# A hybrid attention layer on one core: constants, a root and low parts moved between engines and later in their queues

## The chip, the cores and the metric

The kernel runs on one core of a Trainium2 chip. The metric is the device time of one execution in microseconds (us), taken as the median of several runs. The engines are TensorE (PE in the profile; PEld is its weight load), VectorE (DVE), ScalarE (ACT), GpSimd (POOL) and the queue that issues the transfers (SP). Each engine works through its own instructions in order and waits on semaphores for the others.

## The reference

One layer of a transformer with three kinds of attention side by side on the same normalised input of 1024 rows by 1024 columns, float32. Cut to what matters here:

```python
h = rmsnorm(x, norm_w) @ w_in                  # split into q, k, v and gates of three mixers
# A, differential attention, 4 heads: two softmax maps per head
a  = probs(q1, k1) - lam * probs(q2, k2)       # causal, with a distance penalty per head
oa = rmsnorm(a @ v, subln_w) * (1.0 - lam_init)
ya = oa * silu(ga)
# B, window of 128, 4 heads, with sinks
# C, sparse attention, 8 heads: compressed blocks, 8 chosen blocks of 64 keys, window of 512
oc = gates[..., 0:1] * o_cmp + gates[..., 1:2] * o_slc + gates[..., 2:3] * o_win
return rmsnorm(x + concatenate([ya, yb, yc]) @ w_out, final_norm)
```

## The kernel before

The program is a row of stages, each with its own instructions on every engine: start (normalisation and the first projections), `diff_phase` (A), `swa_phase` (B), the compressed branch of C, `nsa_phase` (window and chosen blocks of C, the last attention stage), and `out_phase` (output projection). Stages end with all engines together.

**High and low parts.** A float32 operand X of a matmul is held as a high part (X rounded to the matmul's format, made by ScalarE) and a low part (X minus the high part). Who makes the low part is a choice between VectorE and GpSimd.

**diff_phase.** A unit n is one head h and one block of 128 query rows; there are 32, eight to a head, and `pos` is n modulo 8. The blocks of a head come in the order 7, 3, 6, 2, 5, 1, 4, 0, so that the units of a head have 8, 4, 7, 3, 6, 2, 5, 1 key tiles of 128. For unit n, TensorE makes two score maps (`scores(n, 0)`, `scores(n, 1)`), VectorE adds the distance penalty and takes the negated maximum (`add_bias`, L837), ScalarE takes the exponentials (L775), VectorE combines both maps (`mix`, L846 to L849: a reciprocal, a small product, one scaled copy, one combination), TensorE transposes the result (`turn`, L657), ScalarE and VectorE copy it out in high and low parts (L785, L857), and TensorE multiplies with the values. Beside this, the `Filler` runs a quarter of an input projection in each unit up to unit 27: twelve matmuls of 512 columns (L169 to L171) whose weights come through a ring of two slots. Its weights are split by ScalarE (L146) and by `split_low` on GpSimd (L153), eight times in the stage: once at the beginning and after every fourth unit from n = 1. At `pos` 1 to 4 the stacks of the next head are made: ScalarE writes the high part (L768), VectorE the low part of the queries at `pos` 1 and 3 (L824), GpSimd the low part of the keys at `pos` 2 and 4 (L902).

TensorE's order in unit n is: `scores(n+2, 0)`, a quarter of the projection, `turn(n)`, `values(n-1)`, `scores(n+2, 1)`. VectorE's is: `add_bias(n+2, 0)`, `low_part(n)`, `mix(n+1)`, `add_bias(n+2, 1)`, then a stack. `scores(n, m)` waits until `add_bias(n-1, m)` has read the bank.

**nsa_phase.** A unit is a head, a branch and a block of query rows; there are 128, first eight of the window branch (at most five tiles), then eight of the chosen blocks (up to eight tiles), and so on. TensorE: `scores(n+2)`, `turn(n)`, `values(n-2)`; VectorE: `add_bias(n+2)` (L1668), `low_part(n)` (L1677); ScalarE: the exponential of unit n+1 (L1602), then `high_part(n)` (L1612). `scores(n)` waits for `add_bias(n-2)`. The first unit that uses the block mask (`n_blocks`), the second key stack (`stack(1)`: L1587 on ScalarE, L1642 on VectorE) and the full bias is n = 8. Ahead of its loop ScalarE has:

```python
exponentials(0)
stack(1)
act.wait_ge(consts_in, CONSTS)      # five transfers: bias, mask, sub-norm row, two gate tiles
nc.scalar.copy(blk[:, :], blk_in[:, :]).then_inc(mask_ready, 1)
```

The sub-norm of A is worked off in pieces in this stage: GpSimd squares (L1723), VectorE sums (L1648), ScalarE takes the root after unit 16 (L1596), VectorE the reciprocal after unit 18 (L1653, L1654), GpSimd scales (L1727, L1730).

## Time and profile before

| | |
|---|---|
| median of 3 runs | 933.0 us (932.86 to 935.32) |
| profiled execution, its own time | 934.59 us |
| its span, first to last instruction | 932.5 us |
| TensorE busy | 835.9 us (90%) |
| VectorE busy | 568.5 us (61%) |
| ScalarE busy | 432.5 us (46%) |
| GpSimd busy | 171.4 us (18%) |
| mean granted clock of TensorE | 0.946 |

Busy time is the time in which an engine has an instruction under way; the shares are means over stages that have different limits. In a group of instructions the number behind the x is how many there are; behind the first bar stand their busy time in us and the mean ns of one, behind the second the idle time of that engine just before them and what ended most of it. In a timeline the first two columns are start and duration in us, and a bracket at the end of a row is the idle time of the engine before it and what ended it. The granted clock is 1.00 at 2.4 GHz and 0.50 at 1.2 GHz.

### The profile page before, as it was taken

Reading aid. Unit: us, or ns where it says so; the run is one execution under the profiler, and the core shown is the slowest. Engines: PE = TensorE matmul, PEld = TensorE weight load, DVE = VectorE, ACT = ScalarE, POOL = GpSimd, SP = SyncE. Lnnn points to the kernel's source line nnn. Section 1 sums busy time; section 2 is a strip of 40 time slices with the busy share of each in tenths; the row PEclk is TensorE's granted clock in tenths of the full one; section 3 lists DMA queues with packets and bytes.
Section 4 is the critical chain, followed back from the end, with each engine's and each line's share of the span. In section 5 each row is a group of like instructions: output and inputs, shape, how many; then the busy total and the mean of one; then the engine's idle time right before and its main releaser. Section 6 shows DMA issues by size and latency. Waiting matters only on the chain. (4 is left out here: it accounts for less than half of the span.)

```text
span 932.5 us, 19153 instructions
## 1 busy us (share of the span) xinstructions
PE 835.9 (90%) x7748; PEld 706.9 (76%) x7748; DVE 568.5 (61%) x1305; ACT 432.5 (46%) x969; POOL 171.4 (18%) x123
## 2 busy tenths in 40 slices
PE   3999999969898888689889993989999999979997
PEld 3899887757686767578778872878887988868885
DVE  4841111136989888567639982878787877843332
ACT  5621111034565555357433322677777787732221
POOL 0233000030312231021045310141010323031220
PEclk9999999989899999699979995999999999979999
DMA  7220226052314122061254316000001111032431
GB/s 267 101 114 1 73 97 169 12 148 82 97 64 123 36 91 69 27 174 44 68 134 107 91 46 174 2 2 2 3 2 47 47 48 47 3 113 94 133 135 45
DMA packets 31942, 73.04 MB, mean 78 GB/s; under 512 B 5104, under 2 KB 13680, under 8 KB 30832
## 3 DMA queue, kind: packets, MB, share of 16 engines
q1 hardware_dynamic: 31856, 71.83, 24.8%
q8 instruction: 61, 1.00, 0.5%
q14 instruction: 25, 0.20, 0.1%
HBM read 55.57 MB, written 16.25 MB: 77 GB/s over the span
## 5 line engine op out<-in xcount | busy, mean ns | idle before, releaser
L1677 DVE SCALAR_TENSOR_TENSOR n_probsT_low<-n_turned,n_probsT_high 128x512 f16<-128x512 f32 (+3 forms) x192 | 94.4, 520 | 32.1 <-ACT n_probsT_high L1612 29.8
L1602 ACT ACTIVATE n_probs<-n_probs,n_negated_max 128x640 f32<-128x640 f32 (+7 forms) x128 | 94.0, 734 | 26.4 <-DVE n_negated_max L1668 25.7
L1612 ACT ACTIVATE n_probsT_high<-n_turned 128x512 f16<-128x512 f32 (+3 forms) x192 | 81.1, 457 | 37.7 <-PE n_turned L657 35.4
L657 PE MATMUL n_turned<-identity,n_probs 128*128 128x128 f32 x528 | 82.2, 280 | 16.1 <-ACT n_probs L1602 15.7
L1770 PE MATMUL n_scores<-w_and_keys_high,stacks 128*128 128x256 f32 (+2 forms) x192 | 78.5, 409 | 3.9 <-DVE n_negated_max L1668 2.5
L657 PEld LDWEIGHTS n_turned<-identity,n_probs 128*128 128x128 f32 x528 | 61.0, 143 | 23.7 <-ACT n_probs L1602 17.9
L153 POOL TENSOR_TENSOR w_and_keys_low<-w_raw,w_and_keys_high 128x1024 fp32r<-128x1024 f32 x15 | 38.2, 2546 | 154.1 <-ACT w_and_keys_high L146 153.9
L1771 PE MATMUL n_scores<-w_and_keys_low,stacks 128*128 128x256 f32 (+2 forms) x192 | 63.2, 336 | 0.0
L1668 DVE CUSTOM_DVE_ANT_0 n_probs<-n_scores,n_bias_full 128x1024 f32<-128x1024 f32 (+3 forms) x64 | 48.3, 754 | 20.0 <-PE n_scores L1774 19.9
L580 PE MATMUL nat<-stacks,xT_high 128*128 128x256 f32 (+1 forms) x192 | 56.0, 292 | 2.8 <-DVE stacks L452 2.6
L785 ACT ACTIVATE a_probsT_high<-a_turned 128x512 f16<-128x512 f32 (+3 forms) x48 | 21.8, 489 | 74.0 <-PE a_turned L657 74.0
L581 PE MATMUL nat<-stacks,xT_high 128*128 128x256 f32 (+1 forms) x192 | 55.2, 287 | 0.0
L582 PE MATMUL nat<-stacks,xT_low 128*128 128x256 f32 (+1 forms) x192 | 55.1, 287 | 0.0
L1969 PE MATMUL o_acc<-stacks,o_yT_high 128*128 128x512 f32 x128 | 51.8, 404 | 2.7 <-POOL o_yT_low L1942 2.7
L1745 POOL TENSOR_TENSOR branches_b_c<-branches_b_c,n_out 128x512 f32<-128x512 f32 x16 | 20.4, 1274 | 179.9 <-DVE n_out L1689 179.9
L169 PE MATMUL a_projected<-xT_high,w_and_keys_high 128*128 128x512 f32 x128 | 52.2, 408 | 0.7 <-ACT staged L179 0.7
L170 PE MATMUL a_projected<-xT_low,w_and_keys_high 128*128 128x512 f32 x128 | 52.0, 406 | 0.0
L171 PE MATMUL a_projected<-xT_high,w_and_keys_low 128*128 128x512 f32 x128 | 51.7, 404 | 0.0
L1970 PE MATMUL o_acc<-w_out_low,o_yT_high 128*128 128x512 f32 x128 | 50.9, 398 | 0.0
L1971 PE MATMUL o_acc<-stacks,o_yT_low 128*128 128x512 f32 x128 | 50.9, 398 | 0.0
L775 ACT ACTIVATE branches_b_c<-branches_b_c,a_negated_max 128x1024 f32<-128x1024 f32 (+7 forms) x64 | 49.4, 774 | 0.4 <-DVE a_negated_max L837 0.4
L665 PE MATMUL n_outp<-values_b_and_selected,n_probsT_high 128*128 128x64 bf16 x864 | 48.6, 193 | 0.0
(266 smaller groups left out, 2540.8 us busy)
## 6 DMA issues: line engine op xcount, KB each, us to landing
w_raw<-in_w_feat SPq DMA_DIRECT2D x23, 512.0 KB, 3.7
features<-staged SPq DMA_DIRECT2D x30, 256.0 KB, 2.0
a_raw<-features SPq DMA_DIRECT2D x36, 128.0 KB, 2.7
s_raw<-features SPq DMA_DIRECT2D x18, 256.0 KB, 4.3
branches_b_c<-in_x SPq DMA_DIRECT2D x8, 512.0 KB, 5.1
silu_gates<-staged SPq DMA_DIRECT2D x16, 256.0 KB, 2.0
gatesT<-silu_gates SPq DMA_DIRECT2D x8, 512.0 KB, 5.4
keys_and_w_out_raw<-in_w_out SPq DMA_DIRECT2D x4, 1024.0 KB, 4.8
```

The lines of the kernel that those rows point to most:

```text
L169: self.nc.tensor.matmul(bank[:, :], a, self.xh[:, k, cols], start=(k == 0), stop=False)
L170: self.nc.tensor.matmul(bank[:, :], a, self.xl[:, k, cols], start=False, stop=False)
L580: nc.tensor.matmul(nat[n % 4][:, 0:cols], xh[:, k, part], a[:, k, 0:cols], start=(k == 0), stop=False)
L581: nc.tensor.matmul(nat[n % 4][:, 0:cols], xh[:, k, part], b[:, k, 0:cols], start=False, stop=False)
L582: mm = nc.tensor.matmul(nat[n % 4][:, 0:cols], xl[:, k, part], a[:, k, 0:cols], start=False, stop=(k == KT - 1))
L657: mm = nc.tensor.transpose(dst[:, j, :], src[:, c:c + P], ident[:, :])
L1602: nc.scalar.activation(pr[:, n % PS, 0:w], pr[:, n % PS, 0:w], ACT.Exp, scale=-1.0, bias=nmax[:, hb % 4, qt:qt + 1], accum_out=sums[:, hb ...
L1612: nc.scalar.activation(pth[:, g % GS, 0:k, :], tp[g % TS][:, 0:k, :], ACT.Copy, scale=PSCALE).then_inc(t_high, 1)
L1677: nc.vector.scalar_tensor_tensor(out=ptl[:, g % GS, 0:k, :], in0=tp[g % TS][:, 0:k, :], scalar=PSCALE, in1=pth[:, g % GS, 0:k, :], op0=ALU ...
L1770: nc.tensor.matmul(out, q, kh[br][:, keys], start=True, stop=False)
L1771: mm = nc.tensor.matmul(out, q, kl[br][:, keys], start=False, stop=not masked)
L1969: nc.tensor.matmul(acc[n % 4][:, :], yh[:, i % 2, k, :], wh[:, k, cols], start=(k == 0), stop=False)
```

## The change

It has four parts. (1) In `diff_phase` GpSimd has no work left: its eight `split_low` become `split_low_on_vector`, the first ahead of everything VectorE does in the stage, the others at the end of the unit after the one in which ScalarE splits; its six key stacks become `stack_keys`, at the end of units with `pos` 2 and 4, on VectorE. (2) In `nsa_phase` ScalarE goes straight into its loop; `stack(1)` moves behind unit 1 (on VectorE too) and the mask copy behind unit 4. (3) The transfers that the mask copy waits for are three instead of five: the two gate tiles count to the semaphore of the output weights, and mask, bias and sub-norm row are issued ahead of the loads of the last two key stacks. (4) The square root on ScalarE and the reciprocal on VectorE go; VectorE makes the reciprocal root by an integer estimate and three Newton steps, twelve instructions on 128x32 elements, after unit 16.

```diff
--- before.py
+++ after.py
@@ -144,6 +145,14 @@
             act.wait_ge(self.sig.loaded, 16 * (self.loads + j - 1))
             act.wait_ge(self.sig.done, self.before + 2 * (j - 1))
         self.nc.scalar.copy(self.ring.hi[:, (self.first + j) % 2, :, :], self.ring.raw[:, :, :]).then_inc(self.sig.high, 1)
+
+    def split_low_on_vector(self, dve, j):
+        if not self.has(j):
+            return
+        s = (self.first + j) % 2
+        dve.wait_ge(self.sig.high, self.splits + j)
+        self.nc.vector.tensor_tensor(self.ring.lo[:, s, :, :], self.ring.raw[:, :, :],
+                                     self.ring.hi[:, s, :, :].bitcast(F32), ALU.subtract).then_inc(self.sig.low, 1)
 
     def split_low(self, pool, j):
         if not self.has(j):
@@ -824,6 +833,12 @@
                 nc.vector.scalar_tensor_tensor(out=low, in0=raw_of(j)[A_QK:2 * A_QK, :], scalar=A_QK ** -0.5 / slope4(h),
                                                in1=low.bitcast(F32), op0=ALU.mult, op1=ALU.subtract).then_inc(q_ready, 1)
 
+            def stack_keys(j):
+                h, m = j // LOADS, j % LOADS // 2
+                dve.wait_ge(stack_high, j + 1 - LOADS)
+                low = ks[2 * A_QK:K, 2 * (h % 2) + m, :]
+                nc.vector.tensor_tensor(low, raw_of(j)[2 * A_QK:K, :], low.bitcast(F32), ALU.subtract).then_inc(k_ready, 1)
+
             def add_bias(n, m):
                 w = len(tiles[n]) * P
                 at = score_layout(len(tiles[n]))[0]
@@ -858,6 +873,7 @@
                                                    in1=pth[:, g % GS, 0:k, :], op0=ALU.mult,
                                                    op1=ALU.subtract).then_inc(t_low, 1)
 
+            fill.split_low_on_vector(dve, 1)
             lc = Chain(dve, chain)
             dve.wait_ge(lam_loaded, 64)
             for i in range(2):
@@ -892,23 +908,10 @@
                     add_bias(n + 2, 1)
                 if pos in range(1, LOADS, 2) and h + 1 < A_H:
                     stack(LOADS * (h + 1) + pos - 1)
-
-        @block.gpsimd
-        def _(pool):
-            def stack(j):
-                h, m = j // LOADS, j % LOADS // 2
-                pool.wait_ge(stack_high, j + 1 - LOADS)
-                low = ks[2 * A_QK:K, 2 * (h % 2) + m, :]
-                nc.gpsimd.tensor_tensor(low, raw_of(j)[2 * A_QK:K, :], low.bitcast(F32), ALU.subtract).then_inc(k_ready, 1)
-                pool.wait_ge(k_ready, (j + 1 - LOADS) // 2)
-
-            fill.split_low(pool, 1)
-            for n in range(UN):
-                h, pos = n // NT, n % NT
-                if split_at(n):
-                    fill.split_low(pool, split_at(n))
                 if pos in (2, 4) and h + 1 < A_H:
-                    stack(LOADS * (h + 1) + pos - 1)
+                    stack_keys(LOADS * (h + 1) + pos - 1)
+                if n >= 1 and split_at(n - 1):
+                    fill.split_low_on_vector(dve, split_at(n - 1))
 
         @block.tensor
         def _(pe):
...
@@ -1502,9 +1505,10 @@
     PS, TS, GS = 4, 3, 6
     GU = RC * HU
     SLABS = 3
-    CONSTS = 16 * 5
+    CONSTS = 16 * 3
+    MASK_AT = 4
     SPLIT_AT = (GU + 8, GU + 24, 6 * HU + 4)
-    ROOT_AT = 2 * NT
+    RSTD_AT = 2 * NT
     yc = yr[:, 2:6, :].rearrange("p a n -> p (a n)").rearrange("p (t d) -> p t d", t=NT)
     qs, gate = stacks, glog
     with ExitStack() as ctx:
...
@@ -1564,19 +1569,19 @@
 
             sp.dma_start(bw[:, :], dist_win).then_inc(bw_in, 16)
             load_stack(1)
+            sp.dma_start(blk_in[:, :], blocks).then_inc(consts_in, 16)
             sp.dma_start(bf[:, :], dist_full).then_inc(consts_in, 16)
-            sp.dma_start(blk_in[:, :], blocks).then_inc(consts_in, 16)
+            sp.dma_start(sub[:, :], subln.partition_broadcast(P)).then_inc(consts_in, 16)
             load_stack(2)
             load_stack(3)
-            sp.dma_start(sub[:, :], subln.partition_broadcast(P)).then_inc(consts_in, 16)
             for i in range(2):
-                sp.dma_start(gates[:, i, :, :], gate_dram[:, :, i * P:(i + 1) * P].rearrange("k p n -> p k n")).then_inc(consts_in, 16)
+                sp.dma_start(gates[:, i, :, :], gate_dram[:, :, i * P:(i + 1) * P].rearrange("k p n -> p k n")).then_inc(w_loaded, 16)
             sp.wait_ge(k_ready, 3)
             for s in range(SLABS + 1):
                 if s >= 1:
                     sp.wait_ge(w_low, s)
                 sp.dma_start(raw[:, :, :], w_out[s]).then_inc(w_loaded, 16)
-            sp.wait_ge(w_loaded, 16 * (SLABS + 1))
+            sp.wait_ge(w_loaded, 16 * (2 + SLABS + 1))
 
         @block.scalar
         def _(act):
@@ -1587,13 +1592,9 @@
                 nc.scalar.copy(kh[j % 2], raw[:, j % 2, :]).then_inc(stack_high, 1)
 
             def split(s):
-                act.wait_ge(w_loaded, 16 * (s + 1))
+                act.wait_ge(w_loaded, 16 * (2 + s + 1))
                 act.wait_ge(scored, GU if s < 2 else 6 * HU)
                 nc.scalar.copy(stacks[:, 2 * s:2 * s + 2, :], raw[:, :, :]).then_inc(w_high, 1)
-
-            def a_roots():
-                act.wait_ge(a_vector, 3)
-                nc.scalar.activation(arms[:, :], arms[:, :], ACT.Sqrt, scale=small[:, 1:2], bias=small[:, 2:3]).then_inc(a_root, 1)
 
             def exponentials(n):
                 w = len(tiles[n]) * P
@@ -1613,17 +1614,17 @@
                                          scale=PSCALE).then_inc(t_high, 1)
 
             exponentials(0)
-            stack(1)
-            act.wait_ge(consts_in, CONSTS)
-            nc.scalar.copy(blk[:, :], blk_in[:, :]).then_inc(mask_ready, 1)
             for n in range(UN):
                 if n + 1 < UN:
                     exponentials(n + 1)
                 high_part(n)
+                if n == 1:
+                    stack(1)
+                if n == MASK_AT:
+                    act.wait_ge(consts_in, CONSTS)
+                    nc.scalar.copy(blk[:, :], blk_in[:, :]).then_inc(mask_ready, 1)
                 if key_stack_at(n):
                     stack(key_stack_at(n))
-                if n == ROOT_AT:
-                    a_roots()
                 if n in SPLIT_AT:
                     split(SPLIT_AT.index(n))
 
@@ -1649,9 +1650,14 @@
                                         ALU.add).then_inc(a_vector, 1)
 
             def a_rstd():
-                dve.wait_ge(a_root, 1)
-                ch.link(nc.vector.reciprocal(arms[:, :], arms[:, :]))
-                nc.vector.tensor_scalar(arms[:, :], arms[:, :], small[:, 3:4], None, ALU.mult).then_inc(a_vector, 1)
+                v, r, t = arms[:, :], guess[:, 0, :], guess[:, 1, :]
+                ch.link(nc.vector.tensor_scalar(v, v, small[:, 1:2], EPS, ALU.mult, ALU.add))
+                ch.link(nc.vector.tensor_scalar(r.bitcast(I32), v.bitcast(I32), -0.5, 1597463007.0, ALU.mult, ALU.add))
+                for _ in range(3):
+                    ch.link(nc.vector.scalar_tensor_tensor(out=t, in0=v, scalar=-0.5, in1=r, op0=ALU.mult, op1=ALU.mult))
+                    ch.link(nc.vector.tensor_tensor(t, t, r, ALU.mult))
+                    ch.link(nc.vector.scalar_tensor_tensor(out=r, in0=t, scalar=1.5, in1=r, op0=ALU.add, op1=ALU.mult))
+                nc.vector.tensor_scalar(v, r, small[:, 2:3], None, ALU.mult).then_inc(a_vector, 1)
 
             def add_bias(n):
                 w = len(tiles[n]) * P
@@ -1691,21 +1697,21 @@
 
             add_bias(0)
             add_bias(1)
-            stack(1)
             ch.link(nc.vector.tensor_scalar(small[:, 0:1], lam_size[:, :], 1.0 / PSCALE, None, ALU.mult))
             ch.link(nc.vector.tensor_tensor(small[:, 1:2], small[:, 0:1], small[:, 0:1], ALU.mult))
             ch.link(nc.vector.tensor_scalar(small[:, 1:2], small[:, 1:2], 1.0 / HD, None, ALU.mult))
-            ch.link(nc.vector.tensor_scalar(small[:, 3:4], small[:, 0:1], 0.5 * (1.0 - LAM_INIT), None, ALU.mult))
-            nc.vector.memset(small[:, 2:3], EPS).then_inc(a_vector, 1)
+            ch.link(nc.vector.tensor_scalar(small[:, 2:3], small[:, 0:1], 0.5 * (1.0 - LAM_INIT), None, ALU.mult))
             for n in range(UN):
                 if n + AHEAD < UN:
                     add_bias(n + AHEAD)
                 low_part(n)
+                if n == 1:
+                    stack(1)
                 if key_stack_at(n):
                     stack(key_stack_at(n))
                 if n in (NT, NT + NT // 2):
                     a_sums((n - NT) // (NT // 2))
-                if n == ROOT_AT + 2:
+                if n == RSTD_AT:
                     a_rstd()
                 if n % NT == 2 and n > NT:
                     write_out(n // NT - 1)
...
```

The order of VectorE's instructions in `diff_phase` around the end of unit 2, before the change. `ISA` with `a_scores` is `add_bias`; `a_probsT_low` is `low_part`; the four rows from the reciprocal are `mix(4)`.

```order
L837 ISA branches_b_c,a_negated_max<-a_scores,a_bias 128x768
L837 ISA a_negated_max 128x1
L837 ISA branches_b_c,a_negated_max<-a_scores,a_bias 128x256
L837 ISA a_negated_max 128x1
L857 SCALAR_TENSOR_TENSOR a_probsT_low<-a_turned,a_probsT_high 128x384
L846 RECIPROCAL a_sums<-a_sums 128x2
L847 TENSOR_TENSOR a_sums<-a_sums,a_lam 128x2
```

The same place in the changed kernel:

```order
L852 ISA branches_b_c,a_negated_max<-a_scores,a_bias 128x768
L852 ISA a_negated_max 128x1
L840 TENSOR_TENSOR stacks<-a_raw,stacks 32x1024
L154 TENSOR_TENSOR w_and_keys_low<-w_raw,w_and_keys_high 128x1024
L852 ISA branches_b_c,a_negated_max<-a_scores,a_bias 128x256
L852 ISA a_negated_max 128x1
L872 SCALAR_TENSOR_TENSOR a_probsT_low<-a_turned,a_probsT_high 128x384
L861 RECIPROCAL a_sums<-a_sums 128x2
L862 TENSOR_TENSOR a_sums<-a_sums,a_lam 128x2
```

Two instructions of 1024 columns, the keys' low part and the weights' low part, now stand between `add_bias(4, 1)` and `add_bias(5, 0)`.

The order on ScalarE at the beginning of `nsa_phase`, before the change:

```order
L1602 ACTIVATE n_probs,n_sums<-n_probs,n_negated_max 128x640
L1587 CAST w_and_keys_high<-keys_and_w_out_raw 128x1024
L1618 CAST n_blocks<-n_blocks_in 128x1024
L1602 ACTIVATE n_probs,n_sums<-n_probs,n_negated_max 128x512
L1612 ACTIVATE n_probsT_high<-n_turned 128x512
```

and in the changed kernel, down to the mask copy:

```order
L1603 ACTIVATE n_probs,n_sums<-n_probs,n_negated_max 128x640
L1603 ACTIVATE n_probs,n_sums<-n_probs,n_negated_max 128x512
L1613 ACTIVATE n_probsT_high<-n_turned 128x512
L1613 ACTIVATE n_probsT_high<-n_turned 128x128
L1603 ACTIVATE n_probs,n_sums<-n_probs,n_negated_max 128x640
L1613 ACTIVATE n_probsT_high<-n_turned 128x512
L1592 CAST w_and_keys_high<-keys_and_w_out_raw 128x1024
...
L1613 ACTIVATE n_probsT_high<-n_turned 128x128
L1625 CAST n_blocks<-n_blocks_in 128x1024
L1603 ACTIVATE n_probs,n_sums<-n_probs,n_negated_max 128x640
```

The key stack stands behind unit 1 and the mask copy behind unit 4, the exponential of unit 1 directly behind that of unit 0.

VectorE around unit 16 of `nsa_phase` in the changed kernel (before it, the rows `n_probsT_low` and `n_probs` follow each other directly here, and L1653 and L1654 stand two units later):

```order
L1683 SCALAR_TENSOR_TENSOR n_probsT_low<-n_turned,n_probsT_high 128x128
L1654 TENSOR_SCALAR n_a_rstd<-n_a_rstd,n_a_small 128x32
L1655 TENSOR_SCALAR n_a_rsqrt<-n_a_rstd 128x32
L1657 SCALAR_TENSOR_TENSOR n_a_rsqrt<-n_a_rstd,n_a_rsqrt 128x32
L1658 TENSOR_TENSOR n_a_rsqrt<-n_a_rsqrt 128x32
L1659 SCALAR_TENSOR_TENSOR n_a_rsqrt<-n_a_rsqrt 128x32
...
L1660 TENSOR_SCALAR n_a_rstd<-n_a_rsqrt,n_a_small 128x32
L1674 ISA n_probs,n_negated_max<-n_scores,n_bias_window 128x384
```

The three rows L1657 to L1659 come three times; `add_bias(19)` (the last row) stands behind them all.

## Rows read from the trace of the kernel before

**Rows 1.** Stretches: PE, PEld, DVE, ACT, POOL busy, clock, DMA share, GB/s.

```profile
229.00:378.00 149.00, 130.39 (x1156) 106.57 (x1154) 128.68 (x264) 86.33 (x186) 32.98 (x13) 0.97 0.25 77
580.00:820.00 240.00, 235.56 (x3538) 200.68 (x3539) 191.81 (x490) 181.54 (x452) 44.40 (x22) 0.99 0.06 20
```

**Rows 2.** Groups of TensorE from 229 to 378 us.

```profile
L657 PE MATMUL a_turned<-identity,branches_b_c 128*128 128x128 f32 x122 | 18.6, 280 | 13.6 <-DVE branches_b_c L849 13.6
```

**Rows 3.** Groups of VectorE by shape from 229 to 378 us.

```profile
L847 DVE TENSOR_TENSOR a_sums<-a_sums,a_lam 128x2 f32<-128x2 f32 x27 | 15.8, 583 | 0.9
...
L849 DVE SCALAR_TENSOR_TENSOR branches_b_c<-branches_b_c,a_sums 128x896 f32<-128x896 f32 x4 | 13.0, 3247 | 0.1
...
L824 DVE SCALAR_TENSOR_TENSOR stacks<-a_raw,stacks 32x1024 fp32r<-32x1024 f32 x6 | 7.3, 1214 | 0.2
...
L846 DVE RECIPROCAL a_sums<-a_sums 128x2 f32<-128x2 f32 x27 | 4.3, 161 | 13.9 <-ACT branches_b_c L775 13.9
...
L849 DVE SCALAR_TENSOR_TENSOR branches_b_c<-branches_b_c,a_sums 128x768 f32<-128x768 f32 x4 | 4.1, 1018 | 0.1
```

**Rows 4.** Group of GpSimd by shape from 205 to 390 us.

```profile
L153 POOL TENSOR_TENSOR w_and_keys_low<-w_raw,w_and_keys_high 128x1024 fp32r<-128x1024 f32 x8 | 21.1, 2632 | 87.2 <-ACT w_and_keys_high L146 87.2
```

**Rows 5.** Timeline of GpSimd and VectorE in units 1 and 2.

```profile
233.87 2.38 POOL L153 TENSOR_TENSOR w_and_keys_low<-w_raw,w_and_keys_high 128x1024 fp32r<-128x1024 f32 x1 [24.45 <-ACT w_and_keys_high L146]
...
233.94 3.25 DVE L849 SCALAR_TENSOR_TENSOR branches_b_c<-branches_b_c,a_sums 128x896 f32<-128x896 f32 x1
...
240.94 2.37 POOL L902 TENSOR_TENSOR stacks<-a_raw,stacks 32x1024 fp32r<-32x1024 f32 x1 [4.69 <-ACT stacks L768]
...
241.09 2.23 DVE L847 TENSOR_TENSOR a_sums<-a_sums,a_lam 128x2 f32<-128x2 f32 x1
```

**Rows 6.** Timeline of TensorE: waits in the first, second and fourth head.

```profile
237.25 0.33 PE L657 MATMUL a_turned<-identity,branches_b_c 128*128 128x128 f32 x1 [2.08 <-DVE branches_b_c L849]
...
252.51 0.39 PE L924 MATMUL a_scores<-stacks 96*128 96x256 f32 x1 [0.77 <-DVE a_negated_max L837]
...
256.57 0.33 PE L657 MATMUL a_turned<-identity,branches_b_c 128*128 128x128 f32 x1 [0.93 <-DVE branches_b_c L849]
...
289.00 0.33 PE L657 MATMUL a_turned<-identity,branches_b_c 128*128 128x128 f32 x1 [0.31 <-DVE branches_b_c L849]
...
290.89 0.40 PE L169 MATMUL a_projected<-xT_high,w_and_keys_high 128*128 128x512 f32 x1
...
369.68 0.33 PE L657 MATMUL a_turned<-identity,branches_b_c 128*128 128x128 f32 x1 [2.17 <-DVE branches_b_c L849]
```

**Rows 7.** A stretch behind the first long wait.

```profile
240.00:245.00 5.00, 5.00 (x12) 4.00 (x13) 4.89 (x7) 1.38 (x3) 2.37 (x1) 0.50 0.66 201
```

**Rows 8.** Timelines of SP, ScalarE and TensorE at the beginning of `nsa_phase`.

```profile
562.81 0.43 SPq L1568 DMA_DIRECT2D n_blocks_in<-in_blocks  x1
...
570.84 1.42 SPq L1573 DMA_DIRECT2D gatesT<-silu_gates  x2
...
578.59 1.04 ACT L1618 CAST n_blocks<-n_blocks_in 128x1024 bf16<-128x1024 f32 x1 [10.79 <-DMA gatesT<-silu_gates]
...
580.40 1.11 PE L657 MATMUL n_turned<-identity,n_probs 128*128 128x128 f32 x4 [12.35 <-ACT n_probs L1602]
```

**Rows 9.** Timelines around units 16 to 18 of `nsa_phase`.

```profile
611.41 1.28 ACT L1596 ACT_TABLE_LOAD   x1
...
613.14 1.28 ACT L1602 ACT_TABLE_LOAD   x1
...
612.07 0.55 DVE L1668 CUSTOM_DVE_ANT_0 n_probs<-n_scores,n_bias_window 128x384 f32<-128x384 f32 x1
...
615.41 0.77 PE L657 MATMUL n_turned<-identity,n_probs 128*128 128x128 f32 x5 [2.68 <-ACT n_probs L1602]
...
618.01 0.34 DVE L1653 RECIPROCAL n_a_rstd<-n_a_rstd 128x32 f32<-128x32 f32 x1
618.39 0.24 DVE L1654 TENSOR_SCALAR n_a_rstd<-n_a_rstd,n_a_small 128x32 f32<-128x32 f32 x1
```

9 lines of the change are left out of this document (6 added, 3 removed).

## The prediction

> **What bounds the kernel now.** I read the stretches first, then the waits of the engine that is busiest in them. In both stages that the change touches this is TensorE: from 229 to 378 us (`diff_phase`) it is busy 130.39 of 149 us, from 580 to 820 us (`nsa_phase`) 235.56 of 240 [rows 1]. So what counts is a wait that ends on TensorE, and the cost of added work is what it makes TensorE wait. VectorE is close behind in `diff_phase` with 128.68 of 149 us and has air in `nsa_phase` with 191.81 of 240 [rows 1].
>
> In `diff_phase` nearly all the idle time of TensorE stands before a transposition and is ended by the last instruction of `mix`: 13.6 us [rows 2]. VectorE's groups show why. Four combinations of 896 columns took 3247 ns each, where those of 768 columns took 1018 [rows 3]; a column costs about 1 ns, so 1.15 us would be in line, and 2.1 us are too much. The small product of 128x2 took 583 ns on average in 27, where the reciprocal of the same size took 161 [rows 3]: 27 x 0.42 = 11.4 us too much. The timeline shows where: such an instruction begins just after one of GpSimd (233.94 after 233.87, 241.09 after 240.94) and lasts until that one ends [rows 5]. So VectorE is held up by GpSimd for about 2 us, ten times: four times by the weights' low part and six times by the keys', 4 x 2.1 + 11.4 = 19.8 us. The other weights' low parts fall beside instructions that aren't held up.
>
> At the beginning of `nsa_phase` one wait of 10.79 us on ScalarE, ended by the gate tiles, keeps the exponential of unit 1 back, and TensorE stands still for 12.35 us before `turn(1)` [rows 8]. Mask and gate tiles are issued 8 us apart, at 562.81 and 570.84 [rows 8]. The third place is unit 18: two table loads of 1.28 us on ScalarE, with the root between them, end in 2.68 us of idle TensorE [rows 9].
>
> **Part 1, `diff_phase`: what goes.** The four holds on the 896-column combination show on TensorE in full: 2.08 us at the first, 2.17 at the last [rows 6], the two between alike, 8.5 in all. Of the 13.6 us [rows 2] 5.1 are then left; the six holds on the small product own most of them (0.93 at 256.57 [rows 6]), and I take 4. The clock: behind the first long wait TensorE ran five microseconds at 0.50, that is 1.2 GHz, while over 149 us the mean is 0.97 [rows 1, 7]. Where it was slow with no wait between, half of the time comes back; the mean says 0.03 x 149 = 4.5 us below full clock, and I take 4, with 0 as the lower bound, since the slow stretch may come at another wait. Together 16.5 us.
>
> **Part 1: what comes.** Fourteen instructions of 1024 columns on VectorE; the nearest row is the queries' low part, 1214 ns [rows 3], so 17.0 us, against 19.8 that go. They are bounded between nothing seen on TensorE (VectorE idles 13.9 us before the reciprocal of `mix` alone [rows 3], waiting for ScalarE) and all 17.0. The first stands ahead of everything, while VectorE still waits for the transfer of the lambda vectors, and costs nothing (1.2 if they came at once). For the rest, what is queued behind them is `add_bias(n+3, 0)`, and TensorE waits for it with `scores(n+4, 0)`. The trace has this case: at `pos` 3 the single low part of the queries stands at that place and TensorE waited 0.77 us [rows 6]. At `pos` 2 two stand there (2.43 us). Counted from the end of `mix(3)`, VectorE needs 1.0 for add_bias(4,1) (768 columns, as the combination of that size [rows 3]), 2.43, and 0.4 for the 256 columns of add_bias(5,0): 3.8 us. TensorE spends 1.9 us from the turn of such a unit to the next projection (289.00 to 290.89 [rows 6]), 0.3 of it on the scores in question, and starts the turn perhaps 0.6 after `mix`, because the projection ahead isn't done: 2.2 us. So it waits 1.6. By the same count, at `pos` 4 the small unit that follows hides the keys' part nearly (0.1), at `pos` 6 the weights' part should cost 0.5, and at `pos` 1 the queries' part, until now hidden by the hold before it, adds 0.3. That is 2.5 us a head for three heads, and 0.5 in the fourth, which has no keys to stack: 8.0 us. Net for part 1: 16.5 - 8.0 = 8.5 us gained; bounds 16.5 - 17.0 = -0.5 and 16.5. GpSimd's instructions of 2.4 to 2.6 us [rows 4, 5] are nowhere waited for by themselves; SP's next load into the ring waits for the low part, which now comes a unit later, but the split that needs it is three units away.
>
> **Parts 2 and 3, the beginning of `nsa_phase`.** The three transfers that count have no wait ahead of them on SP and were issued by 563 us, with only the small row added; ScalarE asks for them after unit 4, some 10 us later. So the wait of 10.79 us goes, and the whole 12.35 us of TensorE [rows 8] with it, since unit 1 is ready when `scores(3)` ends. What comes back: ScalarE's key stack and mask copy (1.04 us each by the copy in [rows 8]) and VectorE's key stack (1.2) now lie between units. `turn(n)` needs an exponential that is made a unit ahead, which hides ScalarE's part; VectorE's delays `add_bias(4)` and with it the exponential of unit 4, which I put at 0.4 us. If that cover were gone, 1.0 + 1.0 + 1.2 = 3.3 us would show. Gain 12.0, bounds 9.1 and 12.4, and up to 1.5 more if TensorE comes back to 2.4 GHz sooner.
>
> **Part 4, the root.** ScalarE loses 1.28 + 0.41 + 1.28 us (613.14 - 611.41 + 1.28 = 3.0 in all [rows 9]), and TensorE's 2.68 us go. VectorE gets twelve instructions for two. One of 128x32 took 0.24, the reciprocal 0.34 us [rows 9], the smallest ones 0.16 [rows 3]: 1.9 to 4.1 us, and I take 12 x 0.25 = 3.0. Here the cover is thin: behind the twelve stands `add_bias(19)`, which began at 612.07 [rows 9], and a unit lasts only 240 / 127 = 1.9 us [rows 1]. With the root gone, `turn(18)` starts about 2.65 us earlier, at 612.8, and TensorE then asks with `scores(21)`, after a turn of five tiles and the values, at about 613.9 (an estimate) for an `add_bias(19)` that ends at 612.07 + 3.0 + 0.55 = 615.6: 1.8 us of waiting in place of 2.68. Gain 0.9 - 0.3 for what VectorE has to catch up + 0.2 for the two instructions gone from unit 18 = 0.8; bounds 0 (4.1 us) and 2.7 (1.9 us, hidden).
>
> The Trainium skill prices a switch of tables higher: "ScalarE: Activation LUTs", section "What ACT_TABLE_LOAD costs", has about 1283 ns for the load and 1380 ns more to drain. The loads here took 1.28 us, and the next instruction stands right behind each, so the trace shows no drain; by the page, part 4 would give up to 2.8 us more, and the sum goes by the trace.
>
> **Sum.** 8.5 + 12.0 + 0.8 = 21.3 us. From the profiled execution's 934.6 us that is 913.3. That execution was 1.6 us above the median, so in terms of the medians 933.0 - 21.3 = 911.7, rounded to 912.
>
> **Rivals.**
> - *VectorE becomes the bound of `diff_phase`.* For it: VectorE is busy 128.68 of 149 us already [rows 1], each head now has four more instructions between things TensorE waits for, and if most of their 17 us show, part 1 gives about nothing. Then 933.0 - 12.8 = 920. Against: more is taken off VectorE (19.8) than is put on. Chance 0.20.
> - *The clock adds to the gain.* If TensorE stays at 2.4 GHz through `diff_phase` and the added low parts hide in VectorE's idle 13.9 us, part 1 gives 14 to 16, and the earlier start of `nsa_phase` 1 more: 904. Against: TensorE still has waits of a microsecond and more. Chance 0.14.
> - *The stall in `nsa_phase` only moves.* ScalarE would wait at the mask copy after unit 4 for transfers, or units 2 to 8 would run dry because VectorE waits for ScalarE's key stack. With 4 us left of 12.0 the time is 920. Against: the mask was issued 8 us before the gates that ended the wait [rows 8]. Chance 0.05.
> - *GpSimd isn't what stretches VectorE's instructions.* If the long combinations and products were the cost of those instructions themselves, nothing goes in part 1 (not even the clock), and all 17.0 us come: 933.0 - 12.8 + 17.0 = 937. It decides once less than 4 of the 19.8 us disappear. Against: each long one begins with one of GpSimd and ends with it [rows 5], while the other sizes keep to their columns. Chance 0.04. The Trainium skill ("SBUF — State Buffer", section "Who interferes with whom") says that a VectorE instruction with two inputs in SBUF and a GpSimd instruction that reads SBUF exclude each other, the second one blocked until the first is done; by that rule this rival can't be, and the trace agrees with 3.25 us in place of 1.15.
>
> **How the numbers follow.** My forecast, both stages gaining about as summed, has 0.57; its own range is 907 to 916. To hold 8 in 10 the range takes in the two cases at 920 and most of the one at 904: 904 to 921. Faster by over 0.3%, about 2.8 us and roughly what a measurement of this kernel can tell from no change: all cases but the last, 0.95. Within 0.3%: 0.02, slower: 0.03.
>
> **What would show it.** Right: in `diff_phase` no combination of 896 columns above 1.3 us and no 128x2 product above 0.2; TensorE's waits before `turn` gone at `pos` 2, and new ones of 1 to 2 us before the scores at `pos` 3 or 4, ended by `add_bias`; the stage about 8.5 us shorter. At the beginning of `nsa_phase` no wait over 1 us after the first exponential, and `turn(1)` about 12 us earlier counted from the stage's start. No table loads at unit 17, and a wait of 1 to 2 us on TensorE ended by `add_bias(19)`. Wrong: if the waits on `add_bias` in `diff_phase` add up to more than 12 us, if TensorE's slow stretches there grow, or if ScalarE stands before the mask copy.

## The result and the profile after

The changed kernel takes 902.13 us (median of 4 executions, 897.16 to 905.45), the kernel before 933.88 (median of 4, 932.86 to 935.32). The ratio is 0.9651, with a 95% interval of 0.9611 to 0.9691: 31.8 us less, where I had forecast 21 and no more than 29 (904 to 921 us). The sign and the places were right and the size was not.

The profiled execution took 900.39 us with a span of 898.6 us. Stretches cut at the stage borders, first of the kernel before (start; `diff_phase` from its first scores to its last transposition; `swa_phase` and the compressed branch; `nsa_phase`; `out_phase`). The columns are those of [rows 1].

```profile
0.00:205.90 205.90, 179.35 (x1050) 157.51 (x1050) 69.95 (x152) 54.27 (x96) 28.58 (x54) 0.97 0.33 109
205.90:391.10 185.20, 160.38 (x1317) 131.15 (x1318) 148.75 (x322) 99.17 (x215) 35.34 (x14) 0.92 0.25 75
391.10:560.40 169.30, 154.70 (x1321) 130.03 (x1318) 117.17 (x273) 69.30 (x158) 39.65 (x16) 0.93 0.34 94
560.40:820.90 260.50, 241.87 (x3582) 205.77 (x3583) 196.29 (x503) 185.50 (x457) 44.69 (x22) 0.96 0.11 34
820.90:932.50 111.60, 99.56 (x489) 82.44 (x485) 36.36 (x56) 24.27 (x43) 23.09 (x17) 0.93 0.33 109
```

The same stages of the changed kernel:

```profile
0.00:205.20 205.20, 179.43 (x1050) 157.58 (x1050) 69.96 (x152) 54.28 (x96) 28.59 (x54) 0.97 0.33 109
205.20:377.00 171.80, 153.50 (x1319) 126.99 (x1320) 144.94 (x336) 99.53 (x215) 0.00 (x0) 0.97 0.28 81
377.00:541.70 164.70, 151.14 (x1320) 127.53 (x1317) 115.68 (x273) 68.87 (x158) 40.28 (x16) 0.96 0.36 96
541.70:788.20 246.50, 241.80 (x3581) 205.97 (x3582) 197.70 (x512) 182.38 (x454) 44.72 (x22) 0.98 0.12 36
788.20:898.60 110.40, 97.64 (x489) 80.98 (x485) 36.39 (x56) 24.29 (x43) 23.12 (x17) 0.98 0.33 110
```

The difference by stage is 0.7, 13.4, 4.6, 14.0 and 1.2 us. Two stages are touched by the change and give 27.4; 6.5 us lie in stages whose instructions are the same, and in the two of them that differ most the clock column moves with the length: 0.93 became 0.96, and 0.93 became 0.98.

In `diff_phase`, the group of scores among TensorE's from 229 to 378 us before the change, which stands beside [rows 2]:

```profile
L924 PE MATMUL a_scores<-stacks 96*128 96x256 f32 (+2 forms) x81 | 24.2, 394 | 3.3 <-DVE a_negated_max L837 3.3
```

and both groups of TensorE from 229 to 364 us in the changed kernel, the same work:

```profile
L927 PE MATMUL a_scores<-stacks 96*128 96x256 f32 (+2 forms) x81 | 25.2, 388 | 8.6 <-DVE a_negated_max L852 7.8
L666 PE MATMUL a_turned<-identity,branches_b_c 128*128 128x128 f32 x122 | 18.0, 274 | 0.2
```

and of VectorE by shape, which answer to [rows 3]:

```profile
L840 DVE TENSOR_TENSOR stacks<-a_raw,stacks 32x1024 fp32r<-32x1024 f32 x6 | 7.3, 1218 | 0.2
...
L864 DVE SCALAR_TENSOR_TENSOR branches_b_c<-branches_b_c,a_sums 128x896 f32<-128x896 f32 x4 | 4.6, 1153 | 0.1
L862 DVE TENSOR_TENSOR a_sums<-a_sums,a_lam 128x2 f32<-128x2 f32 x27 | 4.3, 161 | 0.9
```

The combination of 896 columns costs 1153 ns where it cost 3247, the small product 161 where it cost 583. The 13.6 us before transpositions are down to 0.2. The long waits that are left in this stretch all stand before scores and come three to a head. (Behind it, in the last units of the stage, four waits before transpositions remain, as they did before the change.) Each is ended by the `add_bias` that VectorE does behind its low parts. The timeline of TensorE shows the one behind the two parts of `pos` 2 in the first head, the one behind the weights' part of `pos` 6 and, in the next head, the one behind the queries' part of `pos` 1:

```profile
243.36 0.45 PE L927 MATMUL a_scores<-stacks 96*128 96x384 f32 x1 [1.49 <-DVE a_negated_max L852]
...
262.15 0.50 PE L927 MATMUL a_scores<-stacks 96*128 96x512 f32 x1 [0.40 <-DVE a_negated_max L852]
...
277.68 0.39 PE L927 MATMUL a_scores<-stacks 96*128 96x256 f32 x1 [0.73 <-DVE a_negated_max L852]
```

At the beginning of `nsa_phase`, the timelines of TensorE and ScalarE (compare [rows 8]):

```profile
541.75 0.60 PE L1777 MATMUL n_scores<-w_and_keys_high,stacks 128*128 128x384 f32 x1 [1.37 <-PEq L1215]
...
546.84 0.71 ACT L1603 ACTIVATE n_probs<-n_probs,n_negated_max 128x512 f32<-128x512 f32 x1
...
548.97 0.41 PE L666 MATMUL n_turned<-identity,n_probs 128*128 128x128 f32 x1
...
555.95 1.05 ACT L1625 CAST n_blocks<-n_blocks_in 128x1024 bf16<-128x1024 f32 x1
```

The exponential of unit 1 follows at once, `turn(1)` has no wait, and the mask copy no bracket: the last of its three transfers, issued at 544.57 us, took 8.2 us and had landed 3 us before the copy. And around the root, VectorE and TensorE (compare [rows 9]):

```profile
580.56 0.23 DVE L1654 TENSOR_SCALAR n_a_rstd<-n_a_rstd,n_a_small 128x32 f32<-128x32 f32 x1
...
583.23 0.55 DVE L1674 CUSTOM_DVE_ANT_0 n_probs<-n_scores,n_bias_window 128x384 f32<-128x384 f32 x1
...
583.84 0.39 PE L1777 MATMUL n_scores<-w_and_keys_high,stacks 128*128 128x256 f32 x1 [0.99 <-DVE n_negated_max L1674]
```

Twelve instructions take 583.23 - 580.56 = 2.67 us, and the scores of unit 21 wait 0.99 us for `add_bias(19)`.

### The profile page after: what moved, and what is told of

Same layout as the page of the kernel before. It is cut to its first block and busy times, and to the rows that moved or that the text cites. A ratio compares the mean times of both kernels' runs of the same rounds, so it can differ in the third digit from the quotient of the medians.

```text
span 898.6 us, 19147 instructions
## 1 busy us (share of the span) xinstructions
PE 823.5 (92%) x7748; PEld 699.0 (78%) x7748; DVE 564.7 (63%) x1328; ACT 429.3 (48%) x966; POOL 136.7 (15%) x109
## 5 line engine op out<-in xcount | busy, mean ns | idle before, releaser
L1603 ACT ACTIVATE n_probs<-n_probs,n_negated_max 128x640 f32<-128x640 f32 (+7 forms) x128 | 94.1, 735 | 28.2 <-DVE n_negated_max L1674 27.3
L162 POOL TENSOR_TENSOR w_and_keys_low<-w_raw,w_and_keys_high 128x1024 fp32r<-128x1024 f32 x7 | 18.0, 2569 | 218.6 <-ACT w_and_keys_high L147 218.4
L852 DVE CUSTOM_DVE_ANT_0 branches_b_c<-a_scores,a_bias 128x1024 f32<-128x1024 f32 (+7 forms) x64 | 47.1, 753 | 1.6 <-PE a_scores L927 1.3
```

The lines of the kernel that those rows point to most:

```text
L1603: nc.scalar.activation(pr[:, n % PS, 0:w], pr[:, n % PS, 0:w], ACT.Exp, scale=-1.0, bias=nmax[:, hb % 4, qt:qt + 1], accum_out=sums[:, hb ...
```

## The experiments

### One part at a time

`p1_only` is the kernel before with the diff's hunks on `diff_phase` alone.

> The kernel before with part 1 alone: all low parts of diff_phase on VectorE. Theory A (the holds by GpSimd were each worth their full length on TensorE, and the stage alone gives 13 to 14 us as the changed kernel's trace shows): diff_phase from its first scores to its last transposition 13.4 us shorter, ratio to before 0.983 to 0.987. Theory B (my sum of 8.5 us was right, and the rest of the changed kernel's gain is TensorE's clock in untouched stages): 0.990 to 0.992, with untouched stages as before. Under both nsa_phase still has its wait of 10.8 us on ScalarE.

Measured: 916.41 us, ratio 0.9836 (0.9812 to 0.9861) to 932.41. `diff_phase` took 171.4 us against 185.2. The ratio lies in A's range and the interval leaves B's out: part 1 gives about one and a half times the 8.5 us that I had summed. That is by the stage, 12.6 to 13.8 us less than the 184.0 to 185.2 us that it takes in the two profiles of the kernel before; the times differ by 16.0 us, and part of that lies in stages that weren't touched. `nsa_phase` kept its length (259.7 us against 260.5) and its wait (10.73 us on ScalarE).

`start_only` has the queue changes of `nsa_phase` alone:

```diff
-            stack(1)
-            act.wait_ge(consts_in, CONSTS)
-            nc.scalar.copy(blk[:, :], blk_in[:, :]).then_inc(mask_ready, 1)
...
+                if n == 1:
+                    stack(1)
+                if n == MASK_AT:
+                    act.wait_ge(consts_in, CONSTS)
```

> The kernel before with parts 2 and 3 alone: key stack and mask copy later, three transfers awaited instead of five. Theory A: the wait of 12.35 us of TensorE goes and about 0.4 comes back, 12 us, ratio 0.986 to 0.988; the 2.68 us before unit 18 stay. Theory B (clock helps as well, since the slow stretch of 23.9 us around the stall shrinks to some 10): 13 to 14 us, 0.985.

Measured: 918.51 us, ratio 0.9870 (0.9838 to 0.9902); `nsa_phase` 249.2 us, 11.3 less than in the first profile of before. The wait of 2.68 us before unit 18 stayed, as expected. A fits the stage; the times alone can't tell A and B apart.

`root_only` has the root by Newton steps alone.

> The kernel before with part 4 alone: the reciprocal root by twelve instructions of VectorE. Theory A (the 2.68 us wait for the table loads goes, a wait of about 1 us for add_bias(19) comes): 1.7 us gained, ratio 0.998. Theory B (prediction): 0.8 us gained. Rival: the twelve instructions cost as much as the loads, ratio 1.000.

Measured: 927.70 us, ratio 0.9956 (0.9935 to 0.9977); `nsa_phase` 258.6 us, 1.9 less. The wait for `add_bias` in place of the 2.68 us was

```profile
611.62 0.39 PE L1770 MATMUL n_scores<-w_and_keys_high,stacks 128*128 128x256 f32 x1 [1.34 <-DVE n_negated_max L1669]
```

so 1.3 us net by the waits. The stage doesn't tell more: with the instructions of the kernel before it took 259.7 to 263.1 us in four profiles (`before`, `before_again`, `p1_only`, `weights_only`). The interval of the times is 2 to 6 us and lies above all three expectations, A's included; the waits don't account for that, and how far the clock does (below) stays open. The three ratios multiplied give 0.9665, near the 0.9651 of all together: within the noise the parts add up.

`weights_only` is part 1 with the six key parts left on GpSimd.

> The kernel before with only the weights' low parts of diff_phase on VectorE, the keys' still on GpSimd. Theory A (each hold goes with its own GpSimd instruction): the four combinations of 896 columns fall from 3.25 to 1.15 us, the six products of 128x2 stay near 2 us; 8.5 us of TensorE's waits go and the weights' parts add about 1 us a head: 5 to 7 us gained, ratio 0.993 to 0.995. Rival (the long instructions are VectorE's own cost): all stay long, ratio above 1.

Measured: 923.03 us, ratio 0.9902 (0.9878 to 0.9927), `diff_phase` 175.1 us. VectorE by shape from 229 to 366 us:

```profile
L861 DVE TENSOR_TENSOR a_sums<-a_sums,a_lam 128x2 f32<-128x2 f32 x26 | 9.7, 374 | 0.9
...
L863 DVE SCALAR_TENSOR_TENSOR branches_b_c<-branches_b_c,a_sums 128x256 f32<-128x256 f32 x3 | 5.8, 1929 | 0.1
...
L863 DVE SCALAR_TENSOR_TENSOR branches_b_c<-branches_b_c,a_sums 128x896 f32<-128x896 f32 x4 | 4.6, 1152 | 0.1
```

The combinations of 896 columns are short again. Of the six holds by the keys' parts, A had expected all on the products: about three are there (the mean is 374 ns, not 583), and the other three fell on the combinations of 256 columns, which took 485 ns before. So each hold goes with its own GpSimd instruction, as A says, and what it meets depends on the timing. The gain, 10.1 us of the stage against the first profile of the kernel before, is above A's 5 to 7, and so is the gain by the times, since A's ratio began at 0.993. By single profiles the weights' parts give about three quarters of what part 1 gives, and the keys' the rest.

### Is it GpSimd, and is it its reading?

Two kernels put idle work back on GpSimd in the changed kernel. It works on columns of `ya` that are written later, and is released by the same semaphores as the low parts were:

```diff
+            def extra():
+                nc.gpsimd.tensor_tensor(spare, spare, spare, ALU.subtract).then_inc(spared, 1)
+                done[0] += 1
+                pool.wait_ge(spared, done[0])
```

In `after_writers` the subtraction is replaced by two `nc.gpsimd.memset(spare, 0.0)`, one after the other.

> The changed kernel with twelve idle subtractions put back on GpSimd in diff_phase, 128x1024 on scratch columns, released by the same semaphores as the low parts that were there (the first and the last are left out). Nobody waits for them before head 2 is written. Theory A (a GpSimd instruction that reads SBUF holds up VectorE's instruction with two SBUF inputs): combinations of 896 columns or products of 128x2 stretch by 1.5 to 2 us again, nine times, and diff_phase is 8 to 12 us longer than the changed kernel's 171.7 us. Rival B (what helped was shorter low parts and the other order, not GpSimd's silence): no stretch, diff_phase within 1 us of 171.7.

> As after_readers, but each idle subtraction is two fills with zero of the same columns, which read nothing. Theory A1 (it is the reads that collide; this is also what the Trainium skill says in SBUF - State Buffer, section Who interferes with whom): no product or combination stretches while a fill runs, diff_phase stays at 172 us. Rival A2 (any GpSimd instruction holds VectorE up): stretches of about a fill's length, diff_phase 5 to 12 us longer.

Measured for `after_readers`: 916.05 us, ratio to the kernel before 0.9835 (0.9800 to 0.9871) where the changed kernel has 0.9651; `diff_phase` 187.0 us, 15.2 more than the changed kernel's 171.8 and longer than that of before. I had expected 8 to 12. Of the 15.2 us TensorE is idle for 9.2 and busy for 6.0, at a clock of 0.94 in place of 0.97. A GpSimd and a VectorE row of the timeline, and VectorE's groups:

```profile
231.16 1.90 POOL L924 TENSOR_TENSOR branch_a<-branch_a 128x1024 f32<-128x1024 f32 x1 [27.09 <-ACT w_and_keys_high L147]
...
231.23 2.77 DVE L867 SCALAR_TENSOR_TENSOR branches_b_c<-branches_b_c,a_sums 128x896 f32<-128x896 f32 x1
```

```profile
L843 DVE TENSOR_TENSOR stacks<-a_raw,stacks 32x1024 fp32r<-32x1024 f32 x6 | 9.8, 1637 | 0.2
L867 DVE SCALAR_TENSOR_TENSOR branches_b_c<-branches_b_c,a_sums 128x896 f32<-128x896 f32 x3 | 8.3, 2773 | 0.1
L865 DVE TENSOR_TENSOR a_sums<-a_sums,a_lam 128x2 f32<-128x2 f32 x23 | 7.8, 340 | 0.8
```

Measured for `after_writers`: 901.35 us, ratio 0.9682 (0.9647 to 0.9716), `diff_phase` 171.9 us, with twelve pairs of fills that overlap the same stretches:

```profile
L927 POOL MEMSET branch_a<- 128x1024 f32 x12 | 11.7, 978 | 0.7
L925 POOL MEMSET branch_a<- 128x1024 f32 x12 | 11.6, 968 | 107.5 <-ACT w_and_keys_high L147 69.9 <-ACT stacks L779 37.6
```

```profile
L868 DVE SCALAR_TENSOR_TENSOR branches_b_c<-branches_b_c,a_sums 128x896 f32<-128x896 f32 x4 | 4.6, 1151 | 0.1
L866 DVE TENSOR_TENSOR a_sums<-a_sums,a_lam 128x2 f32<-128x2 f32 x26 | 4.2, 161 | 0.9
```

That settles who holds VectorE up. GpSimd subtractions whose result nobody uses, which read SBUF, bring the loss back (1.90 us of it make a combination of 1.15 into 2.77), and as much time of fills, which only write, costs nothing. That the reads make the difference is what the Trainium skill says in "SBUF — State Buffer", section "Who interferes with whom", and the trace agrees; the two kernels alone don't prove it, since a fill is also another operation and half as long (0.97 us against 1.98). A GpSimd instruction with a single input wasn't tried.

### Can the waits that are left be had?

`root_later` puts the root after unit 27 (`RSTD_AT = 3 * NT + 3`).

> The changed kernel with the twelve instructions of the root after unit 27 of nsa_phase instead of unit 16, where units have up to eight tiles and last longer. Theory A (the 0.99 us wait of TensorE for add_bias(19) is thin cover): the wait goes, no other over 0.5 us comes, nsa_phase 0.5 to 1 us shorter than 246.5, ratio to the changed kernel about 0.999, not to be told by the times alone. Rival: GpSimd's two long scalings, which come later now, fall beside VectorE's instructions and cost it as much.

Measured: 899.32 us, ratio 0.9656 (0.9623 to 0.9690). `nsa_phase` took 245.4 us against 246.5, and the longest wait of TensorE around the root is 0.29 us. As A says, and too little to be seen in the times.

`behind_bias` moves all low parts of the stage behind the next `add_bias`:

```diff
                 if n + 2 < UN:
                     add_bias(n + 2, 0)
+                late = pos - 1
+                if late in range(1, LOADS, 2) and h + 1 < A_H:
+                    stack(LOADS * (h + 1) + late - 1)
+                if late in (2, 4) and h + 1 < A_H:
+                    stack_keys(LOADS * (h + 1) + late - 1)
+                if n >= 2 and split_at(n - 2):
+                    fill.split_low_on_vector(dve, split_at(n - 2))
                 low_part(n)
```

> The changed kernel with every low part of diff_phase (queries, keys, weights) moved behind the next unit's first add_bias, so that none stands ahead of what TensorE's scores wait for. Theory A (TensorE's waits of 0.72, 1.49 and 0.40 us a head are add_bias made late): they go, mix comes later by less than that since VectorE idles before it, diff_phase 4 to 6 us shorter than 171.7, ratio to before about 0.960. Rival (VectorE is the bound of the stage by now): the waits move to the transpositions, diff_phase within 1.5 us of 171.7.

Measured: 902.15 us, ratio 0.9676 (0.9641 to 0.9711), `diff_phase` 172.3 us: no gain, where A had 4 to 6 us. The waits on `add_bias` went, and in their place TensorE waited in each of three heads for the weights' low part itself:

```profile
243.84 0.50 PE L178 MATMUL a_projected<-xT_high,w_and_keys_high 128*128 128x512 f32 x1 [1.66 <-DVE w_and_keys_low L154]
```

I had moved the weights' part past the projection that needs it. `spread` takes this back: one part to a place, the weights' part no later than in the changed kernel.

> The changed kernel with the low parts of diff_phase one to a place: the weights' part behind the first add_bias of the next unit (as early as in the changed kernel, since TensorE waited 1.66 us for it when it came a unit later), the keys' and the second queries' part a unit later, behind the first add_bias as well. Theory A (TensorE's waits of 1.49 and 0.40 us a head come from two parts in one place and from standing ahead of add_bias): these go, the 0.72 stay or shrink, diff_phase 3 to 6 us shorter than 171.7. Rival (VectorE bounds the stage by now): within 1.5 us of 171.7, with waits at the transpositions instead.

Measured: 902.11 us, ratio 0.9696 (0.9671 to 0.9721), `diff_phase` 172.5 us. The 1.49 and 0.40 are gone, and these stand there, in each head alike:

```profile
276.80 0.39 PE L929 MATMUL a_scores<-stacks 96*128 96x256 f32 x1 [0.73 <-DVE a_negated_max L852]
...
280.38 0.33 PE L666 MATMUL a_turned<-identity,branches_b_c 128*128 128x128 f32 x1 [0.47 <-DVE branches_b_c L864]
```

and two more: 0.34 us before a later transposition, and the wait in the second of these rows, whose scores begin as VectorE's keys' part ends:

```profile
250.59 1.22 DVE L840 TENSOR_TENSOR stacks<-a_raw,stacks 32x1024 fp32r<-32x1024 f32 x1
...
251.90 0.70 PE L929 MATMUL a_scores<-stacks 96*128 96x512 f32 x2 [0.73 <-issue]
```

The code tells why: the first scores of a head wait for its last key stack, which this kernel makes a unit later. Together 2.3 us a head stand where the changed kernel has 2.6. The rival named the length rightly, within 1.5 us of 171.7. Its reason is shown in part: some of the waits moved to the transpositions (0.47 and 0.34 us), but as long a one (0.73 us) was put in by my own order, as in `behind_bias`. And the clock hides a gain of this size: over the stage TensorE was idle for 2.8 us less than in the changed kernel and busy for 3.45 us more, at 0.95 in place of 0.97. Whether the keys' part in its old place would give a gain wasn't tried.

> spread with the root after unit 27 of nsa_phase as in root_later. If both act alone: diff_phase as in spread, nsa_phase 245.4 as in root_later, against 246.5 in the changed kernel; ratio to the kernel before 0.958 to 0.963.

Measured: 899.68 us, ratio 0.9671 (0.9650 to 0.9692), where I had expected 0.958 to 0.963; `diff_phase` 171.5, `nsa_phase` 245.6 us. Both act alone: the second stage is as in `root_later`, and `diff_phase`, whose code is that of `spread`, took 1.0 us less at a clock of 0.97. Against the changed kernel on the same runs (`after_again`, next) the interval lies lower, but the touched stages account for only 171.8 + 246.6 - 171.5 - 245.6 = 1.3 us of the 4.9 between the medians. The changed kernel itself had 0.9651 at its first measurement. So the times don't show a better version; what the stages show is 1.0 us by the later root.

### How much is the clock's chance?

> The kernel before, unchanged, for a second profile and more times. In the first pair of profiles 6.4 us of the difference lay in stages that the change doesn't touch, with 17 us less of TensorE at 1.2 GHz there. Theory A (where TensorE falls to 1.2 GHz varies from execution to execution): the stage between swa_phase and the compressed branch, 32.5 us in the first profile, takes 27.5 to 31 here as in the other kernels; ratio to before 1.000. Theory B (it is a property of this kernel): 32 us or more again.

> The changed kernel, unchanged, against the same runs. Theory A (the two stages' 27.6 us are the change's, the rest is chance in the clock): untouched stages within 3 us of those of before_again in sum, ratio to before 0.966 to 0.971. Theory B (untouched stages gain 6 us by the change): ratio 0.962 to 0.966.

Measured: the kernel before 934.46 us, ratio to the other executions of before 1.0024 (1.0005 to 1.0043); the changed kernel 904.56, ratio 0.9716 (0.9697 to 0.9735). The first interval leaves out 1 for one and the same kernel, and the second doesn't overlap the 0.9611 to 0.9691 of the first measurement of the same change. So the intervals are narrower than what a repetition gives, and differences of a few tenths of a percent are not to be read. The stages of `before_again` between start and `out_phase`:

```profile
204.40:388.40 184.00, 155.83 (x1317) 127.47 (x1318) 148.77 (x322) 99.26 (x215) 35.44 (x14) 0.95 0.24 76
388.40:556.20 167.80, 153.69 (x1321) 129.20 (x1319) 117.14 (x273) 69.14 (x158) 39.88 (x16) 0.94 0.35 94
556.20:819.30 263.10, 244.34 (x3583) 208.40 (x3584) 196.56 (x503) 185.98 (x457) 44.76 (x22) 0.94 0.11 33
```

and of `after_again`:

```profile
205.60:377.40 171.80, 153.53 (x1318) 126.92 (x1319) 144.95 (x336) 99.48 (x215) 0.00 (x0) 0.97 0.28 81
377.40:546.80 169.40, 154.56 (x1321) 129.78 (x1318) 117.22 (x273) 69.25 (x158) 39.39 (x16) 0.93 0.34 94
546.80:793.40 246.60, 241.53 (x3581) 205.39 (x3582) 197.68 (x512) 182.51 (x454) 44.75 (x22) 0.98 0.12 36
```

This time the untouched middle of the changed kernel is the longer one, 169.4 us at a clock of 0.93 against 167.8 at 0.94. All three untouched stages together take 486.8 and 483.9 us in the two profiles of before, 480.3 and 486.5 in those of the changed kernel. The two touched stages take 445.7 and 447.1 against 418.3 and 418.4. So the change is worth 27.3 to 28.8 us by its stages, and the 6.5 us beside them in the first pair were chance. A stretch inside the middle shows it best: from ScalarE's last exponential of `swa_phase` to VectorE's first sum of the compressed branch it was 32.4 us in the first profile of the kernel before, 29.7 in `before_again`, and 32.2 again in `after_again`. Theory A of `before_again` holds in this. Theory A of `after_again` holds by the stages (the untouched ones within 2.6 us of each other), its ratio is just above A's 0.966 to 0.971, and B's range is left out.

## Why the prediction was wrong

**The bound and the places: right.** TensorE's waits were what counted, the three places gave the gain, and none of the rivals came as told: no stall moved to the mask copy, nothing got slower. Two things failed, a term of part 1 and the width of the range.

**Part 1 was mis-sized: 8.5 us forecast, 12.2 to 13.4 measured.** The terms can be checked one by one against the stretches from 229 us on. (a) Waits before transpositions: I took 8.5 + 4 = 12.5 to go; 13.6 - 0.2 = 13.4 went. (b) What comes: this is the step that failed most. I counted 8.0 us of new waits before scores, from waits of 1.6 (`pos` 2), 0.1 (4), 0.5 (6) and 0.3 (1) a head. The size was good: they are 1.49, 0.12, 0.40 and 0.73 us, and the long three make 7.8 us in three heads. But I had set them against nothing, while 3.3 us of waits ended by `add_bias` stood there before (the 0.77 of [rows 6] is one of them), and these went too. The group has 8.6 us now, so 5.3 came, not 8.0. (c) The clock: I took 4 us; before, 0.97 over 149 us, now

```profile
229.00:364.00 135.00, 125.34 (x1153) 104.07 (x1151) 122.49 (x275) 86.43 (x184) 0.00 (x0) 1.00 0.27 80
```

with no slow stretch, 4.5 us or a little more. Together 13.4 - 5.3 + 4.5 = 12.6 us, inside what was measured for the stage; the stretch itself became 14.0 us shorter. How the gain divides between waits and clock isn't fixed: over the whole stage TensorE's busy time fell by 6.9 us from the first profile of before to the first of the changed kernel and by 2.3 us in the second pair, its idle time by 6.5 and 9.9 us. The rival in which VectorE becomes the bound took most of 17 us to show, and it didn't come: VectorE's busy time fell (148.75 to 144.94 us). It is true in so far as VectorE ends all long waits that TensorE has left from 229 us on, and the two orders that I tried gained nothing, each with a new wait of its own making.

**Parts 2 and 3: right.** From the first scores of the stage to `turn(1)` it was 580.40 - 560.46 = 19.9 us and is 548.97 - 541.75 = 7.2: 12.7 us, where I had 12.0 with bounds 9.1 and 12.4 and up to 1.5 more by the clock. `start_only` measured 11.3 for the stage. The transfers were no issue.

**Part 4: right in kind, half in size.** 0.8 us forecast. The twelve instructions took 2.67 us, not 3.0, and the new wait was 0.99, not 1.8, so 2.68 - 0.99 = 1.7 us by the waits, and 1.3 in `root_only`. The shorter instructions explain 0.3 of the 0.8 us by which the wait was wrong; the rest lies in my estimate of when TensorE asks. By the Trainium skill ("ScalarE: Activation LUTs", section "What ACT_TABLE_LOAD costs") a switch of tables costs more, an estimate of 2.8 us for the two. The trace doesn't agree. Behind the second load of [rows 9], which ends at 613.14 + 1.28 = 614.42, ScalarE goes on at once:

```profile
614.43 0.83 ACT L1602 ACTIVATE n_probs<-n_probs,n_negated_max 128x640 f32<-128x640 f32 x1
```

**The range.** By the stages the change gives 27.3 to 28.8 us where the sum had 21.3. From the 933.0 us that I started from, this alone makes 904.2 to 905.7, just inside the range of 904 to 921. What took the time out of it, the other 3.0 to 4.5 us of the 31.8, was chance: stages with the same instructions came out shorter, two of the three at a higher clock. I had reasoned on the clock only inside the stages that change, and gave nothing for the others, with three executions of before (2.5 us apart) at hand; over all runs the kernel before lay between 927.7 and 940.2 us. The repeated measurement, 904.56 us, is inside the range by half a microsecond, and that is chance as much.

## What to carry to other kernels

Look for an instruction of VectorE whose mean is far above that of its neighbours in size, and see in the timeline whether it begins inside a GpSimd instruction that reads SBUF: then moving that work to VectorE can relieve VectorE. Look the same way for GpSimd instructions that are too long, inside one of VectorE. A low part that is moved to a later place must still come before the work that needs it. When new waits are estimated at a place, the waits that already stand there have to be taken off. And before a remainder of a gain is explained, compare stages that the change doesn't touch over two profiles of each kernel: here they differed by 6.5 us for the same instructions.

## What the hardware showed unexpectedly

The `out_phase` has the same instructions in all these kernels. In `after_again` it took 111.5 us and in `spread_root` 107.3 us, at clocks of 0.93 and 0.98.

```profile
793.40:904.90 111.50, 99.60 (x489) 82.49 (x486) 36.39 (x56) 24.28 (x43) 23.12 (x17) 0.93 0.33 109
```

```profile
786.10:893.40 107.30, 97.43 (x487) 81.22 (x483) 37.46 (x56) 24.43 (x43) 23.62 (x17) 0.98 0.34 113
```

In other kernels it took 110.4 us at the same 0.98, so the clock isn't all. The traces show the hold of `diff_phase` again, here in both directions. At the beginning of the stage VectorE makes the low part of the output weights (`w_out_low`, 2048 columns) while GpSimd makes that of the first operand (`o_yT_low`, 512 columns), for which TensorE's first projection waits. In the changed kernel, and in twelve of the fourteen profiles in all, VectorE begins first, and GpSimd's instruction takes 2.85 us where the next of the kind takes 1.28:

```profile
793.96 2.29 DVE L1934 TENSOR_TENSOR w_out_low<-keys_and_w_out_raw,stacks 128x2048 fp32r<-128x2048 f32 x1
...
794.52 2.85 POOL L1949 TENSOR_TENSOR o_yT_low<-o_yT,o_yT_high 128x512 fp32r<-128x512 f32 x1 [2.83 <-ACT o_yT_high L1883]
...
797.43 0.50 PE L1976 MATMUL o_acc<-stacks,o_yT_high 128*128 128x512 f32 x1 [3.45 <-POOL o_yT_low L1949]
```

In `spread_root` and `after_readers` GpSimd begins 0.04 us before VectorE, and it is VectorE that is held:

```profile
792.41 1.28 POOL L1951 TENSOR_TENSOR o_yT_low<-o_yT,o_yT_high 128x512 fp32r<-128x512 f32 x1 [2.90 <-ACT o_yT_high L1885]
...
792.45 3.38 DVE L1936 TENSOR_TENSOR w_out_low<-keys_and_w_out_raw,stacks 128x2048 fp32r<-128x2048 f32 x1
...
793.74 0.50 PE L1978 MATMUL o_acc<-stacks,o_yT_high 128*128 128x512 f32 x1 [0.50 <-POOL o_yT_low L1951]
```

TensorE then waits 0.50 us in place of 3.45. Behind the wait of 3.45 us it ran two microseconds at 0.50 and two more at 0.77 (from 798.3 to 802.3 us); behind the 0.50 it ran at 1.00. What turned the order was a slower TensorE: in these two profiles its first transpositions ran at 0.50, and VectorE's second product, which waits for them, came late enough for GpSimd to go first. A kernel that keeps this order on purpose should gain about 3 us, an estimate from 110.4 - 107.3 = 3.1; it wasn't tried.

Twelve idle GpSimd subtractions of 1.98 us lengthened `diff_phase` by 15.2 us, 1.3 us each, where taking away the fourteen GpSimd instructions of the kernel before gave 12.2 to 13.4, 0.9 to 1.0 each, net of what VectorE took over. One reason is that they also held up the low parts that VectorE now makes (1637 ns in place of 1218).
